# MLP down projection: seven block products on three instead of two of the eight pairs of row chunks, ordinary and seven-product pairs by turns

## The reference, cut to what matters

```
u = relu(rms_norm(h, mlp_norm_g) @ w_up)      # (256, 2048) @ (2048, 8192)
h = h + (u * u) @ w_down                      # (256, 8192) @ (8192, 2048)
```

## Time and profile before

| | us |
|---|---|
| median of 3 runs | 2503.82 |
| lowest and highest run | 2503.79, 2504.11 |
| span of the profiled execution | 2504.0 |
| its TensorE busy time | 2480.6 |
| its VectorE busy time | 1753.6 |
| its ScalarE busy time | 1257.8 |

### The profile page before, as it was taken

The page is one execution under the profiler, slowest core; times in us unless marked ns, Lnnn a source line. Parts: engine busy times, 40 slices in busy tenths (PEclk is TensorE's granted clock), DMA queues, the critical chain, the costliest instruction groups (busy, mean ns, idle before and its releaser), DMA issues.

```text
span 2504.0 us, 38061 instructions
## 1 busy us (share of the span) xinstructions
PE 2480.6 (99%) x15416; PEld 2115.6 (84%) x15416; DVE 1753.6 (70%) x1978; ACT 1257.8 (50%) x1506; POOL 29.5 (1%) x26
## 2 busy tenths in 40 slices
PE   9999999999999999999999999999999999999998
PEld 7888888888888888888888888888888888888886
DVE  6656765668668677675777777775776666777777
ACT  7655344544444444445555555544654444444543
POOL 0000000000000000000000000000000000000000
PEclk9999999999999999999999999999999999999999
DMA  9454545546546546555545454556465565556553
GB/s 381 153 183 152 176 153 193 176 164 223 193 161 231 187 171 211 193 195 183 185 153 185 153 185 153 185 170 195 150 217 185 186 200 187 183 194 198 186 188 127
DMA packets 128239, 465.97 MB, mean 186 GB/s; under 512 B 14368, under 2 KB 14624, under 8 KB 127168
## 3 DMA queue, kind: packets, MB, share of 16 engines
q1 hardware_dynamic: 127920, 463.53, 55.2%
q10 hardware_dynamic: 144, 0.02, 0.0%
HBM read 461.39 MB, written 2.10 MB: 185 GB/s over the span
## 4 chain that ended last, share of the span: by engine, by line
PE 94%; issue 4%; DVE 2%; ACT 0%; DMA 0%; SPq 0%; DVEq 0%; POOL 0%; POOLq 0%
PE job L970 30%; PE job L982 16%; PE job L938 11%; PE job L940 11%; PE job L939 11%; PE job L957 2%; PE job L958 2%; PE job L959 2%; PE att L958 2%; PE att L957 2%; PE att L959 2%; PE att L1177 1%; PE att L998 0%; DVE w_low L1593 0%; PE att L1010 0%
## 5 line engine op out<-in xcount | busy, mean ns | idle before, releaser
L1274 ACT ACTIVATE w_high<-raw 128x1024 fp32r<-128x1024 f32 (+1 forms) x883 | 919.6, 1050 | 733.9 <-PE job L940 292.4
L1593 DVE TENSOR_TENSOR w_low<-raw,w_high 128x1024 fp32r<-128x1024 f32 (+1 forms) x883 | 1047.0, 1212 | 310.5 <-ACT w_high L1274 231.0
L970 PE MATMUL job<-actA,w_high 128*128 128x512 f32 x3328 | 798.3, 391 | 0.1
L970 PEld LDWEIGHTS job<-actA,w_high 128*128 128x128 f32 x3328 | 611.8, 188 | 119.9 <-issue 0.7
L982 PEld LDWEIGHTS job<-actA,w_low 128*128 128x128 f32 x3328 | 426.7, 191 | 16.2
L982 PE MATMUL job<-actA,w_low 128*128 128x256 f32 x3328 | 431.7, 283 | 0.0
L1796 DVE TENSOR_TENSOR slots<-job,slots 128x512 f32<-128x512 f32 x102 | 70.5, 691 | 344.1 <-ACT slots L1466 343.5
L938 PE MATMUL job<-w_high,actB 128*128 128x512 f32 x736 | 288.6, 392 | 2.5 <-DVE w_low L1593 2.0
L939 PE MATMUL job<-w_low,actB 128*128 128x512 f32 x736 | 287.1, 390 | 0.0
L940 PE MATMUL job<-w_high,actB 128*128 128x512 f32 x736 | 287.0, 390 | 0.0
L938 PE MATMUL job<-w_high,actA 128*128 128x512 f32 x576 | 230.9, 401 | 0.0
(11 more groups left out here) (257 smaller groups left out, 1906.0 us busy)
## 6 DMA issues: line engine op xcount, KB each, us to landing
raw<-in_weights SPq DMA_DIRECT2D x855, 512.0 KB, 4.2
M<-in_mem_t SPq DMA_DIRECT2D x8, 256.0 KB, 8.0
slots<-in_mem SPq DMA_DIRECT2D x2, 1024.0 KB, 12.2
M<-in_x_t SPq DMA_DIRECT2D x4, 512.0 KB, 13.8
H<-in_x SPq DMA_DIRECT2D x2, 1024.0 KB, 9.0
out<-H SPq DMA_DIRECT2D x8, 256.0 KB, 3.2
slots<-in_w_small SPq DMA_DIRECT2D x1, 1024.0 KB, 9.7
slots<-in_post_mix_g SPq DMA_DIRECT2D x1, 1024.0 KB, 4.3
```

The source lines that it names most:

```text
L970: mm = nc.tensor.matmul(J[job.buf][:, x, :], w_high[:, w % AHEAD, cols], act_both[job.act][:, c, :, :].rearrange("p a t -> p (a t)"), star ...
L1274: nc.scalar.activation(w_high[:, s % AHEAD, cols], raw[:, s % RAW_SLOTS, cols], ACT.Copy)\
L1593: nc.vector.tensor_tensor(w_low[:, s % AHEAD, cols], raw[:, s % RAW_SLOTS, cols], w_high[:, s % AHEAD, cols].bitcast(F32), ALU.subtract).t ...
```

## The change

The order of pairs in a quad job becomes: eight, seven, eight, seven, eight, seven, eight, eight. Three pairs take seven products in place of two. A job now has 22 windows: A0, A1 an eight, A2 to A5 a seven, A6, A7 an eight, A8 to A11 a seven, A12, A13 an eight, A14 to A17 a seven, A18 to A21 two eights. `add_sevens` moves from step A13 of 20 windows to step A17 of 22. The forms of the third seven come from the second projection of a block (j = 1), so `u_forms` runs a second time in each block, on half as much; the forms' tiles grow by half.

```diff
-QUAD_ORDER = (("eight", 2), ("seven", 0), ("eight", 3), ("eight", 4), ("seven", 1), ("eight", 5), ("eight", 6), ("eight", 7))
+QUAD_ORDER = (("eight", 3), ("seven", 0), ("eight", 4), ("seven", 1), ("eight", 5), ("seven", 2), ("eight", 6), ("eight", 7))
 SEVENS = [p for what, p in QUAD_ORDER if what == "seven"]
...
             p.put(job.end, "u_square", j)
             p.put(job.end + 1, "u_split", j)
-            if j == 0:
-                p.put(job.end + 2, "u_forms", b)
+            if j < 2:
+                p.put(job.end + 2, "u_forms", j)
...
-        forms_both = sb("forms_both", [P, 2, 1024], F32R)
+        forms_both = sb("forms_both", [P, 2, 1536], F32R)
...
-        forms, forms_high, forms_low = m_slot(0), forms_both[:, 0, :], forms_both[:, 1, :]
-        form_at = lambda f, p: slice(((f - 1) * 2 + SEVENS.index(p)) * P, ((f - 1) * 2 + SEVENS.index(p) + 1) * P)
+        forms, forms_high, forms_low = Mf[:, 0:1536], forms_both[:, 0, :], forms_both[:, 1, :]
+        form_cols = lambda j: slice(0, 1024) if j == 0 else slice(1024, 1536)
+
+        def form_at(f, p):
+            at = (f - 1) * 2 * P + SEVENS.index(p) * P if p < 2 else 1024 + (f - 1) * P
+            return slice(at, at + P)
...
-                        once("forms_low", job.needs[1] + 1)
+                        once("forms_low", 2 * job.needs[1] + (1 if where < 2 else 2))
...
-                    nc.scalar.activation(forms_high, forms, ACT.Copy).then_inc(S["forms_high"], 1)
+                    cols = form_cols(a[0])
+                    nc.scalar.activation(forms_high[:, cols], forms[:, cols], ACT.Copy).then_inc(S["forms_high"], 1)
...
-                    u = a_slot(2).rearrange("p (q c x t) -> p q c x t", q=2, c=2, x=TT)
+                    j, pairs = a[0], 2 - a[0]
+                    u = a_slot(2 + j).rearrange("p (q c x t) -> p q c x t", q=2, c=2, x=TT)[:, 0:pairs]
...
-                    s1, s2, s3, s4 = (forms[:, i * T:(i + 1) * T].rearrange("p (q t) -> p q t", q=2) for i in range(4))
+                    s1, s2, s3, s4 = (forms[:, form_cols(j)].rearrange("p (f q t) -> p f q t", f=4, q=pairs)[:, f]
+                                      for f in range(4))
...
-                    nc.vector.tensor_tensor(forms_low, forms, forms_high.bitcast(F32), ALU.subtract)\
+                    cols = form_cols(j)
+                    nc.vector.tensor_tensor(forms_low[:, cols], forms[:, cols], forms_high[:, cols].bitcast(F32),
+                                            ALU.subtract)\
                         .then_inc(S["forms_low"], 1)
```

## The result

The changed kernel takes 2522.86 us against 2503.81, a ratio of 1.0078 with a 95% interval of 1.0063 to 1.0092: 19 us slower. The forecast was 2519.4 us, the range 2511 to 2524.

What follows compares the result with a forecast made beforehand. TensorE was taken as the bound, VectorE close behind and longer in A after the change. Three blocks at +3.4 us and +0.3 for the last gave +10.5, plus 5.1 for the clock: +15.6 us, 2519.4 us, range 2511 to 2524.

Steps and rivals of the forecast that it cites:

- TensorE saves 21 matmuls, 4.8 us: Seven quad jobs, each 3 matmuls (0.68 us) shorter by one more seven: 21 matmuls, 4.8 us less on TensorE.
- VectorE becomes the longer one in A: In A and the start of B, a job asks 43.1 us of VectorE against 41.5 us of TensorE.
- the ledger: Step-by-step count of VectorE and TensorE start times through the first block, giving +3.4 us in a block.
- the sign that I gave for it: Expected in the changed profile: VectorE busy for some 42 us in job A.
- The 43.1 us of the prediction: VectorE's time for a job: five eights 11.35, three sevens 23.6, `add_sevens` 5.5, `add_quads` 2.6 us.
- The gap at B2, behind `add_quads`: At B2's start in blocks 0 to 2, TensorE stands still 3.7 us for `add_quads`, losing 3.8 us each.
- The rival of the late loads: Loads at A14 and A20 land 0.9 us later each, 5.4 us over three blocks: about 2524 us; chance 0.13.
- The small waits in A: Two new waits of 0.3 to 0.4 us at the second and third seven's part 1, 0.95 us together.
- The forms at nothing: Second `u_forms` in each block, behind the second projection, costs nothing; without cover up to 4.0 us in each of four blocks.
- The clock falls behind each gap: Behind each of three B2 gaps TensorE runs at half clock for 3.65 us, losing 1.7 us: +5.1 us.
- The last block, +0.3 us: The block without B: two small waits, 0.95 us, less 0.68 us for the matmuls saved.
- the transposes' wait for `add_quads`: In the last block, transposes behind the next job's second window wait for `add_quads`, ending about the same moment: nothing added.

Runs made afterwards that it cites:

- a_only: Changed kernel with three sevens in job A alone, job B in the order of before: 2522.27 us, 1.0074 to the kernel before.
- B alone: Changed kernel with three sevens in job B alone, job A in the order of before: 2502.21 us, 0.9994 to the kernel before.
- quads_first: Changed kernel, on VectorE alone B3's sums and split moved behind A's `add_quads`: 2518.73 us, 1.0060 to the kernel before.
- forms_only: Changed kernel with the old order (two sevens a job); second `u_forms` and larger tiles stay, third seven's forms unused: 2503.69 us, 1.0002 to the kernel before.
- fill_gap: Changed kernel with ten small matmuls of zeros more on TensorE ahead of B2 in three blocks: 2515.61 us, 1.0047 to the kernel before.
- all_later: Changed kernel with each job's order shifted by an eight (two eights first, one last), three sevens by turns: 2523.54 us, 1.0086 to the kernel before.
- b_late: Changed kernel with B's first seven behind two eights and its last two sevens adjacent: 2516.09 us, 1.0048 to the kernel before.
- raw_seven: Changed kernel with seven raw slots for six, second `u_forms` left out, third seven reading the first one's forms: 2515.52 us, 1.0046 to the kernel before.

## Why the prediction was right, and where its terms were off

- **TensorE saves 21 matmuls, 4.8 us.** Right in count.
- **VectorE becomes the longer one in A.** Right in the ledger's sense: from A's sums to `add_quads` its queue is almost never idle. The runs with A alone and B alone show it: A's third seven carries the loss, and B's does not, with the projections behind it. But the sign that I gave for it, VectorE busy for some 42 us in job A, was wrong. Job A of the changed kernel, by stage:

```profile
549.40:593.50 44.10, 42.88 (x185) 33.86 (x183) 37.83 (x44) 22.64 (x25) 0.00 (x0) 1.00 0.47 167
```

VectorE is busy for 37.8 us, no more than the 38.4 of before. The 43.1 us of the prediction hold 3 x 1.13 us of standing still inside the sums, which isn't busy time, and `add_quads` and B's splits ahead of it come only when A is over. A chain that holds another engine up doesn't have to show as a busy share.
- **The gap at B2, behind `add_quads`.** Right in place and cause: `quads_first` moves it to B3. Counted from where the next matmul was due, it costs 4.3, 4.2 and 3.9 us (idle 4.12, 4.01, 3.78), 12.4 in sum; the ledger had 3 x 3.8. It is undersized by 0.3 us a block. In the ledger `add_sevens` starts at 587.2; it started at 586.73 + 1.3 = 588.0. These 0.8 us are A20's split: the ledger has it at 584.8, and it came at 584.34 + 1.3 = 585.6, behind its load. There I had taken the shortest landing, 3.3 us. The rival of the late loads was half true.
- **The small waits in A.** Both are there. They cost 0.3 to 0.6 us each and about 0.9 us a block, the ledger's size. By the sum over the three blocks, 18.2 - 12.4 - 5.8 + 4.1 (18 matmuls saved) = 4.1 us are left for them against 3 x 0.95 = 2.9. Two were not foreseen: a wait of 0.37 us at one of B's sums in block 1, which costs 0.6 us, and in block 0 the start of B, 0.3 us. There `add_sevens` ends so late that B0's split is done at 592.22 + 1.23 = 593.45, and TensorE's matmul, due at 593.4, starts at 593.58. In `a_only` and `quads_first` the same place shows as a wait for that split, of 1.09 and 0.39 us.
- **The forms at nothing.** Right, by `forms_only`.
- **The clock falls behind each gap.** Right in all three. It cost 5.8 us, not 5.1, since in the first block the half clock covers 4.90 us of matmuls. `fill_gap` shows that this term is real and a matter of idleness.
- **The last block, +0.3 us.** Right in the number by luck. The two small waits are there, but the transposes' wait for `add_quads`, which I had put at nothing, is 0.34 us long and costs 0.5: from A4 to the transposes the block is 0.85 us longer (1142.79 - 1101.52 = 41.27 us against 40.42). Behind it TensorE gains 0.5 us back, a little at a time, up to the end of the span, which moved by 0.3 to 0.4.

In sum: predicted 11.4 (gaps) + 5.1 (clock) + 3.8 (small waits) - 4.8 (matmuls) = 15.5; read from the trace 12.4 + 5.8 + some 5 - 4.8 = 18.5; measured 19.

The 0.5 us between 18.5 and 19 are no more than the scatter ahead of the MLP: the first A4 comes at 557.44 us in `a_only`, 557.60 in `forms_only` and 558.26 in the changed kernel. What stays open: why TensorE gains 0.5 us back behind the MLP, and what the three longer executions of `all_later` spent their 4.5 to 11 us on.

## What to carry to other kernels

When a cheaper algorithm moves work from TensorE to VectorE, compare the two engines' time for one job, not their shares over the span: 70% busy over the span hid a stage in which VectorE had 3 us to give and was asked for 5.6. Then look for what stands last in VectorE's queue and frees something that TensorE waits for; here it was one addition behind the next job's sums. A gap on TensorE costs its own length and the half clock behind it, half as much again here, and a few waits of 0.7 us that look too small to matter can be worth more than the 21 matmuls.

## What the runs showed of the hardware that I had not expected

Gaps of nearly one length lowered the clock or didn't. In `b_late` the three gaps are 2.78, 2.83 and 2.70 us; the 5 us behind each:

```profile
623.50:628.50 5.00, 4.96 (x15) 0.66 0.74 267
803.00:808.00 5.00, 5.00 (x22) 1.00 0.73 237
980.70:985.70 5.00, 5.00 (x22) 1.00 0.67 245
```

In `raw_seven`, behind gaps of 3.96, 2.68 and 2.68 us:

```profile
602.10:607.10 5.00, 4.95 (x15) 0.66 0.46 136
781.00:786.00 5.00, 5.00 (x22) 1.00 0.49 133
958.10:963.10 5.00, 4.93 (x12) 0.50 0.47 122
```

Two gaps of 2.68 us in one execution: full clock behind one, half clock over all of the next 5 us behind the other. The second is dearer than any of the changed kernel's: 14 matmuls take 6.12 us from 958.17 to 964.29, 2.95 more than at 0.227 us each. `all_later` had full clock behind 3.20 us and a fall behind 3.02. Taken together, in `quads_first`, `raw_seven`, `b_late` and `all_later` 15 gaps in the MLP were 2.38 to 3.25 us long; the clock fell behind 6 of them. Behind all seven gaps of 3.6 to 4.1 us (the changed kernel, `a_only`, `raw_seven`) it fell, and in the kernel before it fell 1.3 us after the end of a gap of only 1.99 us. So in this kernel the length alone doesn't say what a gap of 2 to 3.3 us costs beyond itself: 0 to some 3 us.
